# Storing and reloading split weights in the convolutional feed-forward stage of a hybrid decoder step

## What is computed

```
mixed = ga * (h_m @ w_a) + gb * (h_a @ w_b)
x = x + mixed @ w_out                       # "branch" and "out" products
y = conv_ffn(rmsnorm(x, g_ffn), ...)

def conv_ffn(xn, buf, w_up, w_conv, b_conv, w_down):
    u = xn @ w_up                           # 1024 -> 2 * 2816
    ext = concatenate([buf, u], axis=1)
    c = b_conv + sum_over_3_taps(w_conv[tap] * ext[:, tap:tap + S])
    a, g = split(c, 2)
    return (gelu(a) * g) @ w_down           # 2816 -> 1024

x = rmsnorm(x + y, g_final)
```

## Time and profile before

| | us |
|---|---|
| median of 3 runs | 2944.92 (2944.90 to 2948.83) |
| the profiled execution | 2944.33 |
| its span in the trace | 2942.4 |

### The profile page before, as it was taken

The page is one execution under the profiler, slowest core; times in us unless marked ns, Lnnn a source line. Parts: engine busy times, 40 slices in busy tenths (PEclk is TensorE's granted clock), DMA queues, the critical chain, the costliest instruction groups (busy, mean ns, idle before and its releaser), DMA issues. The chain is left out here.

```text
span 2942.4 us, 47347 instructions
## 1 busy us (share of the span) xinstructions
PE 2786.9 (95%) x17306; PEld 2651.6 (90%) x17306; DVE 1929.2 (66%) x3032; ACT 1460.2 (50%) x2776; POOL 460.6 (16%) x663
## 2 busy tenths in 40 slices
PE   8999999999999999999899999989999997999996
PEld 8888898989998899999899999889999987999996
DVE  4222257676767578888877777676666657666775
ACT  4222235454555455555544554764445586444563
POOL 2111112111111122222100000030000012111112
PEclk9999999999999999999999999999999999999998
DMA  5643356556555387776533333344333344333333
GB/s 181 209 134 129 113 191 194 177 183 224 187 159 160 112 263 263 265 265 210 177 128 122 129 122 119 128 154 138 107 104 115 106 134 164 115 104 104 108 105 70
DMA packets 310327, 454.10 MB, mean 154 GB/s; under 512 B 43538, under 2 KB 190546, under 8 KB 310098
## 3 DMA queue, kind: packets, MB, share of 16 engines
q1 hardware_dynamic: 307986, 450.94, 47.6%
q10 hardware_dynamic: 2112, 0.13, 0.0%
HBM read 346.12 MB, written 105.88 MB: 154 GB/s over the span
## 5 line engine op out<-in xcount | busy, mean ns | idle before, releaser
L2410 ACT ACTIVATE f_wh<-both_high 128x512 fp32r<-128x512 f32 (+1 forms) x766 | 465.9, 619 | 553.1 <-PE f_ps L2328 521.9
L2323 PE MATMUL f_ps<-f_xt,f_wh 128*128 128x348 f32 (+1 forms) x3696 | 675.9, 325 | 67.1 <-ACT f_ps L2484 46.4
L2646 DVE TENSOR_TENSOR f_wl<-both_high,f_wh 128x512 fp32r<-128x512 f32 (+1 forms) x766 | 545.3, 721 | 283.3 <-ACT f_wh L2410 280.8
L2323 PEld LDWEIGHTS f_ps<-f_xt,f_wh 128*128 128x128 f32 x3696 | 604.1, 190 | 85.4 <-ACT f_ps L2484 61.1
L2323 PE MATMUL f_ps<-f_gbuf,f_wh 128*128 128x348 f32 (+1 forms) x2112 | 386.1, 323 | 17.6 <-DVE both_low L2848 6.4
L2328 PE MATMUL f_ps<-f_xt,f_wl 128*128 128x348 f32 (+1 forms) x1848 | 372.2, 323 | 0.0
L2323 PEld LDWEIGHTS f_ps<-f_gbuf,f_wh 128*128 128x128 f32 x2112 | 342.8, 189 | 26.6 <-DVE both_low L2848 11.2
L2328 PEld LDWEIGHTS f_ps<-f_xt,f_wl 128*128 128x128 f32 x1848 | 310.4, 189 | 0.0
L829 PE MATMUL pp<-gxh,gwh 128*128 128x416 f32 x792 | 291.4, 368 | 1.3 <-DVE gxl L778 1.3
L829 PE MATMUL pp<-gxh,gwl 128*128 128x416 f32 x792 | 279.8, 353 | 0.0
L829 PE MATMUL pp<-gxl,gwh 128*128 128x416 f32 x792 | 278.5, 352 | 0.0
(11 more groups left out here) (342 smaller groups left out, 4460.5 us busy)
## 6 DMA issues: line engine op xcount, KB each, us to landing
...
both_high<-up_sums SPq DMA_DIRECT2D x176, 256.0 KB, 2.7
...
```

The costliest lines, as they stand in the source:

```text
L2323: pe.matmul(out, cut(wh, k), x(k), start=(start and k == 0 and x is xhi), stop=False, skip_group_check=not start or not stop)
L2410: act.activation(ring_slot(wh, e, w), src, ACT.Copy).then_inc(ev("w_hi"), 1)
L2646: dve.tensor_tensor(ring_slot(wl, e, w), src, ring_slot(wh, e, w).bitcast(F32), ALU.subtract).then_inc(ev("w_lo"), 1)
```

## The change

The second halves of the ring are now kept in DRAM. In pair 0 SP stores, for each sum s1 to s4 of each tile and for each `down` slice, both halves from the ring (`store_parts`) in place of the sum alone. In pairs 1 and 2 these chunks are no longer loaded raw and split: SP loads both halves straight into the ring (`load_parts`), as soon as PE is through the product six chunks back, and PE waits for the loads (`hi_in`, `lo_in`). The chunks a11, a12, a22 are split as before. ACT's iteration now begins with the seeds and `c12`, then `w_high`, then the posts; gelu, `high` and `low` of a tile that is followed by another tile stand two iterations later; `taps1` waits for the product of the tile before instead of its low half. The `out` units of the last span are seeded and read back by ACT. The third ACT copy of the input split (`prep_sums_high`) moves one iteration later. The column sum of a pair's end uses two banks. `mixed_high` stands ahead of the seeds and gates.

```diff
@@ -1777,7 +1777,7 @@
 BANKS_C, BANKS_D = 6, 3
-STAT = 7
+STATS = (7, 6)
 SEEDED = 4
@@ -1864,6 +1864,35 @@
+def whole_product(v):
+    kind, n, i = PLAN[v]
+    return kind == "down" or kind == "q" and PRODUCTS[i][0][0] == "s"
+def pair_at(v):
+    kind, n, _ = PLAN[v]
+    return n if kind == "down" else n // FT
+STORED = [whole_product(v) and pair_at(v) == 0 for v, _ in CHUNK]
+LOADED = [whole_product(v) and pair_at(v) > 0 for v, _ in CHUNK]
+SPLITS, STORES, LOADS = [], [], []
+for _e in range(len(CHUNK)):
+    _old = _e - RING
+    SPLITS.append((SPLITS[-1] if _e else 0) + (not LOADED[_e]))
+    STORES.append((STORES[_old] if _old >= 0 else 0) + STORED[_e])
+    LOADS.append((LOADS[_old] if _old >= 0 else 0) + LOADED[_e])
+def chunk_of_pair(e):
+    v, _ = CHUNK[e]
+    kind, n, i = PLAN[v]
+    return FIRST[AT["down", 0, i]] if kind == "down" else QC[n % FT][i]
 def split_until(v):
@@ -1884,7 +1913,7 @@
         v = behind(n)
-        steps = (("c12", "taps1"), ("taps0",), ("product",), ("high",), ("low",))
+        steps = (("c12", "taps1"), ("taps0",), (), (), ("product",), ("high",), ("low",))
         if PLAN[v][0] == "down":
@@ -1895,18 +1924,14 @@
 def seeded(v):
...
     kind, p, i = PLAN[v]
-    return kind == "down" and p < END and i // KT >= SEEDED
-SEEDS = [(v, s) for v in range(len(PLAN)) if seeded(v) for s in range(2)]
+    return kind == "down" and p < END and i // KT >= SEEDED or kind == "out" and p == SPANS - 1
+SEEDS = [(v, s) for v in range(len(PLAN)) if seeded(v) for s in range(len(BANK[v]))]
 SEED_AT = {x: i for i, x in enumerate(SEEDS)}
 SEEDED_AT = {}
-for _v in range(len(PLAN)):
-    if seeded(_v):
-        for _s in range(2):
-            _w = _v - 1 if _s else _v - 2
-            _w = (_w, 0) if _s else (_w, 1)
-            SEEDED_AT.setdefault(_w, []).append((_v, _s))
+for _v, _s in SEEDS:
+    SEEDED_AT.setdefault((_v - 1, 0) if _s else (_v - 2, 1), []).append((_v, _s))
...
 def ahead_of_ffn(scratch):
@@ -2070,6 +2096,17 @@
+    def part_rows(e):
+        v, _ = CHUNK[e]
+        kind, n, i = PLAN[v]
+        return (downs[i], PARTS[i // KT] * P) if kind == "down" else (ups[tile_of(n), int(PRODUCTS[i][0][1]) - 1], QUAD)
+    def slot_stored(engine, e):
+        if e >= RING:
+            wait(engine, f"part_out{e % RING}", 32 * STORES[e - RING])
     ring_slot = lambda t, e, w=QUAD: t[:, QUAD * (e % RING):QUAD * (e % RING) + w]
@@ -2115,6 +2152,9 @@
                 issue.setdefault(max(v - 4, 0), []).append(("unit", v))
+            continue
+        if LOADED[e]:
+            issue.setdefault(CHUNK[e - RING][0] + 1, []).append(("parts", e))
             continue
@@ -2126,8 +2166,9 @@
     store_at = {}
-    for v, items in sums_at.items():
-        store_at.setdefault(v + 1, []).extend(items)
+    for e in range(len(CHUNK)):
+        if STORED[e]:
+            store_at.setdefault(next(v for v in range(len(PLAN)) if split_until(v) > e) + 1, []).append(e)
...
     def _(sp):
@@ -2151,31 +2192,36 @@
             if old >= 0:
-                wait(sp, "w_lo", QC[old][j] + 1)
+                wait(sp, "w_lo", SPLITS[QC[old][j]])
             elif name in ("a11", "a12", "s3"):
...
                 wait(sp, "h_lo", KT)
-            if n - 1 < FT and n > 0:
+            if 0 < n <= FT:
                 if name == "a11":
...
                     wait(sp, "sum_ready", 4 * (n - 1) + 4)
-            if name[0] == "s":
-                wait(sp, f"{name}_out", 16 * min(n, FT))
             halves_of = {"a11": (0, 0), "a12": (0, QUAD), "s3": (1, 0), "a22": (1, QUAD)}
-            if name[0] == "s" and n >= FT:
-                src = sums[r, int(name[1]) - 1]
-            else:
-                s, c0 = halves_of[name]
-                src = a["w_up"][r, s][:, c0:c0 + QUAD]
-            sp.dma_start(role(n, name), src).then_inc(ev(role_event(n, name)[0]), 16)
-        def store_sum(n, w):
-            sp.wait_ge(ev("sum_ready"), sum_done(n, w))
-            sp.dma_start(sums[tile_of(n), w - 1], slot[f"s{w}"]).then_inc(ev(f"s{w}_out"), 16)
+            s, c0 = halves_of[name]
+            sp.dma_start(role(n, name), a["w_up"][r, s][:, c0:c0 + QUAD]).then_inc(ev(role_event(n, name)[0]), 16)
+        def store_parts(e):
+            rows, w = part_rows(e)
+            sp.wait_ge(ev("w_lo"), SPLITS[e])
+            for h, t in enumerate((wh, wl)):
+                sp.dma_start(rows[h][:, 0:w], ring_slot(t, e, w).bitcast(F32)).then_inc(ev(f"part_out{e % RING}"), 16)
+        def load_parts(e):
+            rows, w = part_rows(e)
+            first = chunk_of_pair(e)
+            sp.wait_ge(ev("mm_done"), DONE[CHUNK[e - RING][0]])
+            slot_stored(sp, e)
+            sp.wait_ge(ev(f"part_out{first % RING}"), 32 * STORES[first])
+            for h, (t, name) in enumerate(((wh, "hi_in"), (wl, "lo_in"))):
+                sp.dma_start(ring_slot(t, e, w).bitcast(F32), rows[h][:, 0:w]).then_inc(ev(f"{name}{e % RING}"), 16)
...
         def heads_in(b):
@@ -2313,10 +2359,17 @@
             cut = lambda t, k: ring_slot(t, e0 + k // 4)[:, P * (k % 4):P * (k % 4) + P]
+            def ready(e, split, load):
+                if LOADED[e]:
+                    wait(pe, f"{load}{e % RING}", 16 * LOADS[e])
+                else:
+                    wait(pe, split, SPLITS[e])
             for lo, hi in ((0, K - last), (K - last, K)):
...
                     if k % 4 == 0:
-                        wait(pe, "w_hi", e0 + k // 4 + 1)
+                        ready(e0 + k // 4, "w_hi", "hi_in")
                     if low:
@@ -2337,10 +2390,10 @@
             wait(pe, "rt_ready", SPANS)
-            wait(pe, f"ps_read{STAT}", used_before(p))
+            wait(pe, "frt_ready", 2 * p)
             for s in range(2):
-                wait(pe, "frt_ready", 2 * p + s)
-                pe.matmul(stp[:, 0:w], ones, facc[:, WIDE * s:WIDE * s + w], start=True, stop=True).then_inc(ev("fst_done"), 1)
+                wait(pe, f"ps_read{STATS[s]}", used_before(p, STATS[s]))
+                pe.matmul(ps[STATS[s]][:, 0:w], ones, facc[:, WIDE * s:WIDE * s + w], start=True, stop=True).then_inc(ev("fst_done"), 1)
@@ -2368,8 +2421,11 @@
                 wait(pe, f"ps_read{n}", BEFORE[v][0])
+                if seeded(v):
+                    wait(pe, "seeded", SEED_AT[v, 0] + 1)
                 product(ps[n][:, 0:TB], FIRST[v], KT, lambda k: mh[:, k, :], lambda k: ml[:, k, :],
-                        low="mixed_lo" if i == 0 else None, at=KT * b, last=2 if i == 0 else 0)
+                        low="mixed_lo" if i == 0 else None, at=KT * b, last=2 if i == 0 else 0,
+                        start=not seeded(v))
             else:
@@ -2403,10 +2459,13 @@
     def _(act):
         def w_high(e):
+            if LOADED[e]:
+                return
             src, w = chunk_source(e)
...
                 wait(act, "mm_done", DONE[CHUNK[e - RING][0]])
+                slot_stored(act, e)
             act.activation(ring_slot(wh, e, w), src, ACT.Copy).then_inc(ev("w_hi"), 1)
...
         def square(b, o):
@@ -2455,6 +2514,9 @@
             act.activation(xth[:, 1:3, k, 0:w], st[:, 1, 0:2 * w].rearrange("p (j t) -> p j t", j=2), ACT.Copy).then_inc(ev("x_hi"), 1)
+        def prep_sums_high(p, k):
+            n, w = 4 * p + k, WIDTH[p]
             act.wait_ge(ev("t_ready"), n + 1)
@@ -2500,29 +2562,36 @@
+        def kept_in(v, s):
+            kind, p, i = PLAN[v]
+            return xspan[p % 2][:, i, :] if kind == "out" else xres[:, i % KT, WIDTH[p] * s:WIDTH[p] * s + WIDTH[p]]
         def seed(v, s):
...
-            _, p, i = PLAN[v]
-            w, o = WIDTH[p], i % KT
-            evacuated(act, AT["down", p, i - KT], s)
-            wait(act, f"ps_read{BANK[v][s]}", BEFORE[v][s])
-            if BANK[v][s] == STAT:
+            kind, p, i = PLAN[v]
+            m, t = BANK[v][s], kept_in(v, s)
+            if kind == "out":
+                act.wait_ge(ev("xr_in"), 16 * sum(len(span_halves(b)) for b in range(SPANS)))
+            else:
+                evacuated(act, AT["down", p, i - KT], s)
+            wait(act, f"ps_read{m}", BEFORE[v][s])
+            if m in STATS:
                 act.wait_ge(ev("rt_ready"), SPANS)
                 wait(act, "frt_ready", 2 * p)
-            act.activation(ps[BANK[v][s]][:, 0:w], xres[:, o, w * s:w * s + w], ACT.Copy).then_inc(ev("seeded"), 1)
+            act.activation(ps[m][:, 0:t.shape[-1]], t, ACT.Copy).then_inc(ev("seeded"), 1)
...
         def unseed(v, s):
-            _, p, i = PLAN[v]
-            w, o = WIDTH[p], i % KT
-            act.wait_ge(ev("mm_done"), DONE[v] - 1 + s)
-            act.activation(xres[:, o, w * s:w * s + w], ps[BANK[v][s]][:, 0:w], ACT.Copy).then_inc(ev(f"ps_read{BANK[v][s]}"), 1)
+            t = kept_in(v, s)
+            act.wait_ge(ev("mm_done"), DONE[v] - (len(BANK[v]) - 1 - s))
+            act.activation(t, ps[BANK[v][s]][:, 0:t.shape[-1]], ACT.Copy).then_inc(ev(f"ps_read{BANK[v][s]}"), 1)
...
         def scaled(n, s):
...
```

(35 more changed lines are left out.)

28 lines of the change are left out of this document (15 added, 13 removed).

## The result

The changed kernel takes 2859.85 us (median, 2858.3 to 2866.84) where the kernel before takes 2945.21 beside it (2944.9 to 2948.83): a ratio of 0.9712, with a 95% interval of 0.9694 to 0.973. The forecast was 2859.5. The total was right. Two of the reasons behind it were not, as the experiments show.

A forecast was written before the change was run, and what follows sets the result against it. After about 1360 us PE mostly bounds the kernel, so only its stalls can be won. Gains 42.2 + 5.6 + 2.5 - 2.0 + 24.2 + 10.9 + 1.4 = 84.8 us, from 2944.3 to 2859.5; range 2838 to 2892.

The forecast's parts named there:

- short units: Seeded short down units at pair ends: fewer splits on ACT and DVE, 0.6 us in pair 0, 1.9 in pair 1.
- (a): Pair 0's tiles: DVE, 98% full, finishes c22 just late, costing 0.3 us in each of 17 tiles, 5.1 us.
- (b): Before down in four runs: PE waits for the hidden tile's low half, 0.75 us each, 3.0 us in all.
- Part 1: ACT's new order and gelu two iterations later: 50.3 us of line 2484 stalls go, 42.2 net of new waits.
- part 2: Halves stored and loaded: 5.6 us from evacuation waits, 2.5 from short units, less 2 charged for blocked SP.
- Part 3: Starts of pairs 1 and 2: two banks end the wait between column sums, c22 mostly stays late; 24.2 us gained.
- Part 4: Last span and pair 0's start: adds moved from DVE to ACT, later gelu; 7.0 and 3.9, together 10.9 us.
- DVE takes over: Rival: DVE's waits for ACT become stalls in pair 0, and pair starts give back the gain; 2883 us, chance 0.18.
- The 2 us charged: DMA cost in pairs 1 and 2: SP blocked by a result or x_rows ahead of a load, ends 0 and 12.

The follow-up runs named there:

- gelu one sooner: Changed kernel with gelu, high and low half one iteration later than in the kernel before, not two: 2855.33 us, ratio 0.9694.
- Seeds first: Kernel before with seeds and c12 ahead of the weight split on ACT, gelu in its old place: 2947.34 us, ratio 1.0005.
- The halves alone: Changed kernel with only stored and loaded halves; ACT order, gelu, single bank, last span and input copies as before: 2897.38 us, ratio 0.9836.
- Spreading the norms: Changed kernel with the last span's reciprocal and scalings spread over three tiles of pair 0, not two: 2863.07 us, ratio 0.971.

## Why the prediction was right, and where it was not

By stages the sum held. The losses give, forecast beside measured:

| | forecast | measured |
|---|---|---|
| last span, start and first two tiles of pair 0 | 10.9 | 8.6 |
| rest of pair 0 | 10.3 | 8.4 |
| starts of pairs 1 and 2 | 24.2 | 23.0 |
| rest of pairs 1 and 2 (seeds, evacuation, DMA) | 35.5 | 36.6 |
| short units | 2.5 | 4.7 |
| end, to the first column sum | none | 2.7 |
| end, from the first column sum on | 1.4 | 1.7 |
| sum | 84.8 | 85.7 |

(10.3 is 18.4 of stalls less the 8.1 of (a) and (b), and 35.5 is 10.2 + 21.7 + 5.6 - 2.0. The measured column is the table above but for the last 1.7, which is 21.0 us less 19.3 to the end of the span; the difference of the two spans is 85.9.)

*Part 1.* Right that the stalls on 2484 go, all of them. A tile in the middle of pair 0 took 13.79 us from start to start, with 13.5 to 13.8 forecast:

```profile
1625.29 1.55 PE L2376 MATMUL f_ps<-f_xt,f_wh 128*128 128x348 f32 x8
...
1639.08 1.55 PE L2376 MATMUL f_ps<-f_xt,f_wh 128*128 128x348 f32 x8
```

(a), `c22`, was forecast at 0.3 us in 17 tiles; it is 0.27 in ten. (b), the low half ahead of `down`, was forecast at 3.0 us and costs 6.3 in four places (2.04, 1.42, 1.62, 1.22). So (a) came to 2.7 us for 5.1 and (b) to 6.3 for 3.0, and their sum, 9.0 for 8.1, is close because the errors cancel. The step of (b) that failed is the estimate that the low half ends 2.4 us into its iteration. One iteration earlier would have been enough, as gelu one sooner shows.

*Part 1 against part 2.* The attribution failed. Part 1 was to bring 42.2 us and brings 33 alone; part 2 was to bring 6.1 and brings 48.7 alone. The step was to charge the stalls of pairs 1 and 2 to the order in which ACT works, with the earlier trace rows, a tile of pair 0, as their cause. In pairs 1 and 2 the split between gelu and the seed, and splits ahead of the taps on DVE, were among those that the loads remove. Either cure takes most of the loss in the rest of pairs 1 and 2 (8.4 to 1.9 or -3.2, and 22.2 to 5.0 or 2.5), but the order puts waits for the low half in their place and leaves the two starts as they were, and the loads shorten the starts too (35.4 to 21.8). The total came out right since a stall that two edits cure was booked once. Seeds first, the edit that the argument of the earlier trace rows is about, brings nothing by itself.

*Part 3.* The size was right, 23.0 against 24.2, and the shares were less so. The two sums now follow each other, as the first row below shows. The forecast put 5.5 us a pair on them, 11.0, and the two banks bring 8.1. The halves alone bring 13.6 (16.1 + 19.3 less 8.8 + 13.0), of which the forecast named only three splits fewer on DVE. What remains is what was named, the reciprocal ahead of `c22`. Rows of the changed kernel, as in the earlier trace rows:

```profile
1921.22 1.33 PE L2396 MATMUL f_ps<-f_nrm,both_low 128*128 128x348 f32 x4
...
1928.67 4.49 DVE L2843 RECIPROCAL f_nrm<-f_nrm 128x696 f32<-128x696 f32 x1
...
1936.87 1.54 PE L2376 MATMUL f_ps<-f_xt,f_wh 128*128 128x348 f32 x8 [2.81 <-DVE both_high L2805]
```

*Part 4.* The sum of 8.6 for 10.9 is in part luck, since 6.9 of it come from a place that the forecast had not listed. In the last span of the kernel before PE waits 4.14 us for ACT's weight split, and ACT reaches that split only after the long copy of the inputs' sums, which waits for DVE:

```profile
1390.77 1.36 ACT L2459 ACTIVATE f_xt<-both_high 128x1392 fp32r<-128x1392 f32 x1 [4.06 <-DVE both_high L2715]
1392.04 1.13 ACT L2410 ACTIVATE f_wh<-both_high 128x512 fp32r<-128x512 f32 x2
...
1392.80 0.69 PE L2323 MATMUL f_ps<-f_mh,f_wh 128*128 128x416 f32 x1 [4.14 <-ACT f_wh L2410]
```

In the changed kernel this copy stands one iteration later, and the stall is gone with it and with the slow restart behind it. The runs in which the copy keeps its old place keep the loss (8.0 to 8.7). `mixed_high` was moved too, and no run moves one of the two alone. At the start of pair 0, 8.8 down to 1.8 was forecast, and 7.1 remains (a wait of 4.13 us, was 6.87). The step that failed is the relief that moving seven adds off DVE was to bring: without them the wait is 6.4 us, so they bring 2.3. The first two tiles won nothing, against 3.9 forecast. Their stall comes from DVE's load there:

```profile
1415.49 2.74 DVE L2764 RECIPROCAL f_rinv<-f_rinv 128x416 f32<-128x416 f32 x1
...
1434.98 2.69 PE L2376 MATMUL f_ps<-f_xt,f_wh 128*128 128x348 f32 x8 [5.51 <-DVE both_high L2805]
```

Here the rival "DVE takes over" was right, in this one place. Spreading the norms bears it out: the first two tiles lose 3 us less and the rest of pair 0 6.7 more.

*DMA.* The 2 us charged were about right: three waits for loads, 1.7 us in all. Two of the signs failed all the same. Landings of the loaded halves were to stay under 8 us, and the longest took 9.0. The rate in the long runs of pairs 1 and 2 is 188 and 182 GB/s, and not above 200: the 241 worked out had taken the heaviest tile for all (the stretches of the earlier trace rows with 114 and 107 and the added 78 give 192 and 185). At the starts it is 273 and 237. The ring order that the Trainium skill states (DMA: Bandwidth & Descriptors, section Queues, rings and completion order) agrees with the 6.8 us from issue to PE's restart behind the residual.
